# Attention keys loaded ahead of the last projections, output weights loaded in halves and rounded two quarters later, and the last gate row loaded at the fourth tile

## The reference, cut to what matters

```python
mod = jnp.einsum('bd,de->be', c, w_ada[l]) + b_ada[l]
sh1, sc1, gt1, sh2, sc2, gt2 = jnp.split(mod, 6, axis=-1)
h = rmsnorm(x, g_norm_mix[l]) * (1.0 + sc1[:, None, :]) + sh1[:, None, :]
x = x + gt1[:, None, :] * hybrid_mixer(h, positions, w_in[l], w_o[l])
h = rmsnorm(x, g_norm_ffn[l]) * (1.0 + sc2[:, None, :]) + sh2[:, None, :]
x = x + gt2[:, None, :] * hier_moe(h, ...)
...
# hybrid_mixer
proj = jnp.einsum('bsd,de->bse', h, w_in)
y_a = dsa_attention(qa, ka, va, qi, ki, wi)      # 8 heads of 64, top 256 keys of a query
y_b = retention(qb, kb, vb, gb, positions)       # 8 heads of 64, by chunks
y = jnp.concatenate([y_a, y_b], axis=-1)
return jnp.einsum('bse,ed->bsd', y, w_o)
```

## Time and profile before

| | |
|---|---|
| median of three runs | 1718.81 us (1712.06 to 1719.7) |
| the profiled execution's own time | 1713.41 us |
| its span | 1711.5 us |
| TensorE busy | 1473.0 us, 86% |
| VectorE busy | 1125.3 us, 66% |
| ScalarE busy | 912.8 us, 53% |
| GpSimd busy | 286.1 us, 17% |
| granted TensorE clock, mean | 0.926 |
| chain that ended last | TensorE 74%, VectorE 11%, DMA 5%, ScalarE 4% |

### The profile page before, as it was taken

The page is one execution under the profiler, slowest core; times in us unless marked ns, Lnnn a source line. Parts: engine busy times, 40 slices in busy tenths (PEclk is TensorE's granted clock), DMA queues, the critical chain, the costliest instruction groups (busy, mean ns, idle before and its releaser), DMA issues.

```text
span 1711.5 us, 21563 instructions
## 1 busy us (share of the span) xinstructions
PE 1473.0 (86%) x7406; PEld 1149.6 (67%) x7406; DVE 1125.3 (66%) x1496; ACT 912.8 (53%) x1228; POOL 286.1 (17%) x212
## 2 busy tenths in 40 slices
PE   3899998999999897778899752999999999999940
PEld 2587445888887785455666542788888888888830
DVE  6633778662267973334444235899999999999936
ACT  4321665879983112324444301677777777777711
POOL 0000100240000001400000001223223232232125
PEclk8899989999999898599999965999999999999975
DMA  9198532222323226112211104999999999999847
GB/s 370 46 340 316 197 131 105 99 99 99 117 71 128 79 68 222 52 50 74 75 50 44 50 25 148 391 397 398 404 399 398 398 398 400 392 403 395 346 163 269
DMA packets 103990, 368.27 MB, mean 215 GB/s; under 512 B 11248, under 2 KB 24176, under 8 KB 79344
## 3 DMA queue, kind: packets, MB, share of 16 engines
q1 hardware_dynamic: 75632, 291.85, 44.7%
q10 hardware_dynamic: 17024, 41.95, 6.4%
q0 software_dynamic: 11264, 33.57, 5.5%
HBM read 306.50 MB, written 69.21 MB: 220 GB/s over the span
## 4 chain that ended last, share of the span: by engine, by line
PE 74%; DVE 11%; DMA 5%; ACT 4%; issue 3%; POOL 2%; SPq 1%; DVEq 0%; POOLq 0%; ACTq 0%
PE PS L1618 19%; PE PS L1620 19%; PE PS L1619 18%; PE PS L1719 3%; PE PS L1920 2%; PE PS L1743 2%; DMA WK<-in_w_ada 1%; PE PS L1829 1%; PE PS L1816 1%; DVE wlo L1541 1%; DVE WK L1045 1%; PE PS L1704 1%; PE PS L1675 1%; DMA BIG<-in_b_sh 1%; PE PS L1895 1%
## 5 line engine op out<-in xcount | busy, mean ns | idle before, releaser
L1541 DVE TENSOR_TENSOR wlo<-raw,whi 128x2048 fp32r<-128x2048 f32 x192 | 435.9, 2286 | 33.9 <-ACT whi L958 33.5
L958 ACT ACTIVATE whi<-raw 128x2048 fp32r<-128x2048 f32 x192 | 363.9, 1914 | 116.2 <-DVE WK L1560 80.8
L1618 PE MATMUL PS<-whi,xhi 128*128 128x512 f32 x512 | 203.8, 398 | 7.3 <-DVE wlo L1541 6.5
L1620 PE MATMUL PS<-whi,xlo 128*128 128x512 f32 x512 | 201.1, 393 | 0.0
L1619 PE MATMUL PS<-wlo,xhi 128*128 128x512 f32 x512 | 200.1, 391 | 0.0
L850 ACT ACTIVATE KV<-ACC,WK 128x1024 int8<-128x1024 f32 (+4 forms) x160 | 147.5, 925 | 29.9 <-DVE WK L1181 27.3
L1618 PE MATMUL PS<-KVR,BIGR 128*128 128x512 f32 x320 | 127.7, 399 | 5.9 <-DVE KVR L1107 5.9
L699 POOL COPY wcol<-tw 128x1 f32 (+1 forms) x32 | 63.0, 1969 | 376.8 <-DVE WK L1578 376.8
L1620 PE MATMUL PS<-KVR,BIGR 128*128 128x512 f32 x320 | 125.4, 392 | 0.0
L1619 PE MATMUL PS<-KVR,BIGR 128*128 128x512 f32 x320 | 125.0, 391 | 0.0
L1618 PEld LDWEIGHTS PS<-whi,xhi 128*128 128x128 f32 x512 | 97.0, 189 | 27.6 <-issue 5.7
(11 more groups left out here) (322 smaller groups left out, 2966.3 us busy)
## 6 DMA issues: line engine op xcount, KB each, us to landing
raw<-in_w_gate SPq DMA_DIRECT2D x64, 1024.0 KB, 7.8
raw<-in_w_up SPq DMA_DIRECT2D x64, 1024.0 KB, 7.8
raw<-in_w_down SPq DMA_DIRECT2D x64, 1024.0 KB, 7.2
y_dram<-zero ACTq DMA_DIRECT2D x8, 3072.0 KB
WK<-in_w_ada POOLq DMA_DIRECT2D x16, 1024.0 KB, 7.4
y_dram<-WK ACTq DMA_DIRECT2D x32, 512.0 KB
KV<-in_w_in SPq DMA_DIRECT2D x5, 2048.0 KB, 9.8
KV<-in_x SPq DMA_DIRECT2D x16, 512.0 KB, 5.0
```

The source lines that it names most:

```text
L958: nc.scalar.activation(whi[:, slot], raw[:, q], ACT.Copy).then_inc(G("m_hi"), 1)
L1541: V.tensor_tensor(wlo[:, slot], raw[:, q], whi[:, slot].bitcast(F32), ALU.subtract)\
L1618: mm(out_, x_hi, w_hi, start=first, stop=False)
L1620: return mm(out_, x_lo, w_hi, start=False, stop=final)
```

## The change

The keys get the place of the third slot's rounded weights (BIG[20480:24576]), which is free once `ka` is projected, and are loaded in one transfer at step 17; four of the eight rounded slices of `wo` take the keys' old place (`WOR`). The small load of tile 0's keys goes. The output weights come in halves, the second behind `gt1`, and `gt1` has a count of its own; the router's weights move behind the other rows. The first late row stands after quarters 2 and 3 of tile 0 instead of 0 and 1, the second at the first two quarters of tile 1, the third within the first output products. ScalarE rounds slices 4 to 7 in quarters 2 and 3 of tile 0 and 0 to 3 in the first two of tile 1; GpSimd subtracts four slices, VectorE the other four. `gt2` is loaded when the fourth tile begins and made in tile 5. `TILES` is the identity, so the indices that go through it are as before.

```diff
-KEY_PARTS = ((0, 512), (512, 1024))
-KEYS_FROM = {128: 0, 256: 1, 640: 2}
+TILES = (0, 1, 2, 3, 4, 5, 6, 7)
+WO_ORDER = (4, 5, 6, 7, 0, 1, 2, 3)
...
-        wo_hi = [BIGR[:, a:a + 1024] for a in (0, 1024, 2048, 3072, 20480, 21504, 22528, 23552)]
-        kaT = KV[:, 0:4096].rearrange("p (j s) -> p j s", j=4)
+        kaT = BIG[:, 20480:24576].rearrange("p (j s) -> p j s", j=4)
+        wo_hi = [(BIGR, WOR)[k // 4][:, 1024 * (k % 4):1024 * (k % 4) + 1024] for k in range(KD)]
...
-        between[0] = [[("late", m)] for m in range(4)]
-        between[1] = [[("late", 4)], [("late", 5), ("mix", (0, 0))], [("mix", (0, 1))], [("norm", 0)]]
+        between[0] = [[], [], [("late", 0)], [("late", 1)]]
+        between[1] = [[("late", 2)], [("late", 3), ("mix", (0, 0))], [("late", 4), ("mix", (0, 1))],
+                      [("late", 5), ("norm", 0)]]
...
-        between[T - 1][2].append(("late", 6))
-        between[T - 1][3].append(("late", 7))
+        between[5][2].append(("late", 6))
+        between[5][3].append(("late", 7))
... SyncE
+                if step == 2 * T + 1:
+                    for q in range(2):
+                        sp.wait_ge(G(f"st_q{q}"), 16 * T)
+                    sp.wait_ge(G("a_proj"), T * (ATTEND + 2))
+                    sp.dma_start(kaT, k_dram).then_inc(G("ld_k0"), 16)
...
-            for q in range(2):
-                sp.wait_ge(G(f"st_q{q}"), 16 * T)
-            sp.dma_start(keys0, k_dram[:, :, 0:P]).then_inc(G("ld_k0"), 16)
             sp.wait_ge(G("a_proj"), UNITS)
-            for n, (a, b) in enumerate(KEY_PARTS):
-                sp.dma_start(kaT[:, :, a:b], k_dram[:, :, a:b]).then_inc(G(f"ld_k{n + 1}"), 16)
-            sp.dma_start(wo, wo_v).then_inc(G("ld_wo"), 16)
+            sp.dma_start(wo[:, 4:8], wo_v[:, 4:8]).then_inc(G("ld_wo"), 16)
             sp.wait_ge(G("b_y"), T)
-            sp.dma_start(WC["gt1"], b_gt1).then_inc(G("ld_c"), 16)
-            sp.dma_start(WC["wr"], w_router).then_inc(G("ld_c"), 16)
+            sp.dma_start(WC["gt1"], b_gt1).then_inc(G("ld_gt1"), 16)
+            sp.dma_start(wo[:, 0:4], wo_v[:, 0:4]).then_inc(G("ld_wo_last"), 16)
             sp.dma_start(WC["sc2"], b_sc2).then_inc(G("ld_c"), 16)
             sp.dma_start(WC["g"], g_ffn).then_inc(G("ld_c"), 16)
             sp.dma_start(WC["sh2"], b_sh2).then_inc(G("ld_c"), 16)
+            sp.dma_start(WC["wr"], w_router).then_inc(G("ld_c"), 16)
...
-                if i == T - 1:
-                    sp.wait_ge(G("topk_done"), len(SCORED))
+                if i == 3:
                     sp.dma_start(gt2, b_gt2).then_inc(G("ld_gt2"), 16)
... GpSimd
-            for k in range(KD):
-                pool.wait_ge(G("w_hi"), 4 * (ATTEND + 3) + k + 1)
+            for k in range(4, KD):
+                pool.wait_ge(G("w_hi"), 4 * (ATTEND + 3) + WO_ORDER.index(k) + 1)
                 own.go(tt(wo_lo[:, k], wo[:, k], wo_hi[k].bitcast(F32), ALU.subtract), G("wo_lo"))
... ScalarE, at the end of a quarter
-                    if i == 0:
-                        for k in (lo, lo + 1):
-                            act.wait_ge(G("ld_wo"), 16)
+                    quarter = 4 * i + lo // 2
+                    if 2 <= quarter < 6:
+                        for k in WO_ORDER[2 * quarter - 4:2 * quarter - 2]:
+                            act.wait_ge(G("ld_wo" if k >= 4 else "ld_wo_last"), 16)
                             own.go(A(wo_hi[k], wo[:, k], ACT.Copy), G("w_hi"))
... VectorE, at the end of a quarter
+                    quarter = 4 * i + lo // 2
+                    if 4 <= quarter < 6:
+                        for k in (2 * quarter - 8, 2 * quarter - 7):
+                            dve.wait_ge(G("w_hi"), 4 * (ATTEND + 3) + WO_ORDER.index(k) + 1)
+                            own.go(V.tensor_tensor(wo_lo[:, k], wo[:, k], wo_hi[k].bitcast(F32), ALU.subtract),
+                                   G("w_lo"))
                 if kind == "late":
-                    dve.wait_ge(*((G("ld_gt2"), 16) if row == "gt2" else (G("ld_c"), 16 * 5)))
+                    dve.wait_ge(*((G("ld_" + row), 16) if row in ("gt1", "gt2") else (G("ld_c"), 16 * 4)))
... TensorE
                 if lo == 0:
+                    if i == 0:
+                        pe.wait_ge(G("ld_k0"), 32)
                     pe.wait_ge(G(f"ld_q{i % 2}"), 16 * (i // 2 + 1))
-                    if cols_of(i) in KEYS_FROM:
-                        n = KEYS_FROM[cols_of(i)]
-                        pe.wait_ge(G(f"ld_k{n}"), 32 if n == 0 else 16)
```

More of the change, by code:

```diff
@@ L151, in block_kernel @@
         rounded.close()
+        rounded = ExitStack()
+        rounded.enter_context(nc.sbuf_tensor("BIGP", [P, 24576], F32R))
+        WOR = rounded.enter_context(nc.sbuf_tensor("WOR", [P, 4096], F32R))[:, :]
+        rounded.close()
         BIG = sb_before("BIG", [P, 24576])
@@ L509, in load_queries @@
             def load_queries(n):
-                sp.dma_start(queries(n), q_dram[:, :, tile(n)]).then_inc(G(f"ld_q{n % 2}"), 16)
+                sp.dma_start(queries(n), q_dram[:, :, tile(TILES[n])]).then_inc(G(f"ld_q{n % 2}"), 16)
             def store_retained(t):
@@ L1253, in negated_logits @@
                 i = u // HA
-                K = cols_of(i)
-                bias = WC["bias01"][:, 256 - K:256] if i < FIRST_SCORED else ACC[:, ACC_OFF[i]:ACC_OFF[i] + K]
+                n = TILES[i]
+                K = cols_of(n)
+                bias = WC["bias01"][:, 256 - K:256] if n < FIRST_SCORED else ACC[:, ACC_OFF[n]:ACC_OFF[n] + K]
                 b = 2 * (u % 2)
@@ L1360, in _ @@
                     spend(STEP_SPEND, pieces)
-            for _ in pieces:
-                pass
             for kind, i in order:
@@ L1420, in _ @@
                     dve.wait_ge(G("b7_ready"), at7[("route", i, 0)] + 1)
-                    own(V.tensor_copy(L[:, i, :], PS[:, 7, 0:36]), G("b7_free"))
+                    own(V.tensor_copy(L[:, TILES[i], :], PS[:, 7, 0:36]), G("b7_free"))
             dve.wait_ge(G("st_x1"), 16 * T)
@@ L1743, in query_keys @@
                         last = mm(PS[:, 2 * (h % 2) + b, 0:w], queries(i)[rows, h // 2, :],
-                                  (kaT if i else keys0)[rows, h // 2, 512 * b:512 * b + w], start=True, stop=True)
+                                  kaT[rows, h // 2, 512 * b:512 * b + w], start=True, stop=True)
                         if w < 512 or 512 * b + w == K:
@@ L1814, in turn_weights @@
                     pe.wait_ge(G("c_pt"), n - 1)
-                for b in range(4 * g, min(4 * g + 4, i + 1)):
+                for b in range(4 * g, min(4 * g + 4, TILES[i] + 1)):
                     last = tr(PS[:, 4 + n % 2, P * (b % 4):P * (b % 4) + P],
@@ L1829, in values @@
                         last = mm(PS[rows, 6, P * (h // 2):P * (h // 2) + P], va[:, b, HD * h:HD * h + HD],
-                                  PT[(n + h % 2) % 4][:, P * (b % 4):P * (b % 4) + P], start=(b == 0), stop=(b == i))
+                                  PT[(n + h % 2) % 4][:, P * (b % 4):P * (b % 4) + P], start=(b == 0), stop=(b == TILES[i]))
                 last.then_inc(G("c_pv"), 1)
@@ L1881, in _ @@
                         if i == 0 and h == 0:
-                            pe.wait_ge(G("wo_lo"), k + 1)
+                            if k < 4:
+                                pe.wait_ge(G("w_lo"), 4 * (ATTEND + 3) + k + 1)
+                            else:
+                                pe.wait_ge(G("wo_lo"), k - 3)
                         last = split_product(PS[:, 7, :], yhi[:, k, :], ylo[:, k, :], wo_hi[k][:, part], wo_lo[:, k, part],
```

24 lines of the change are left out of this document (12 added, 12 removed).

## The result

| | before | after |
|---|---|---|
| time, median of 4 runs each (us) | 1717.97 (1712.06 to 1719.7) | 1696.29 (1695.42 to 1698.91) |
| the profiled execution's own time | 1713.41 | 1695.42 |
| its span | 1711.5 | 1693.5 |

The ratio is 0.9877, with a 95% interval of 0.9855 to 0.9899: 17 to 25 us less. The two profiled executions are 18.0 us apart.

What follows compares the result with a forecast made beforehand. Bound by bytes in a load queue around tile 0, with a second such place at tile 7. Front 9.7 + tile 7 10.2 - tile 5 1.5 = 18.4 us: 1695.0 profiled, 1700.4 from the median; forecast 1699, range 1690 to 1709.

Steps and rivals of the forecast that it cites:

- Keys at no cost: Retention steps: the early 2 MB key load delays v of step 6 within its slack of 3 us, cost 0.
- The queue: Load queue before tile 0: 6.43 MB instead of 8.53, so rows land at 683.0, gt1 near 672, yb issued about 683.7.
- Lead at the sums of tile 0, 14.0 us: Tile 0, TensorE: the sums of rows start at 688.0 instead of 702.17, about 14.0 us sooner.
- Lead at (mix 0,0), 11.9: First output product, held by VectorE's moved work, starts at 706.3 instead of 718.24, a lead of 11.9 us.
- Late 4 and 5, 2.2: Late rows now behind the first output products cost 2.1 and 0.1 us, leaving a front gain of 9.7.
- Tile 7, 10.2: Gt2's early load removes the wait before tile 7's sums, 9.35 us, plus 0.89 by full clock: mix 10.2 us earlier.
- It also keeps its clock: Tile 7: TensorE stays at full clock, so the sums take 1.09 us instead of 1.98.
- Tile 5, 1.5 (0 to 3.5): Gt2's two late rows, now in tile 5, cost 1.5 us there, between 0 and 3.5.
- Nothing after the first place starts at a fixed time, so the lead is handed on: After the front: each load waits for a tile's count, so the lead reaches the experts undiminished.
- the moved wait: Rival, chance 0.2: subtractions and roundings ahead of late 2 and 3 hold (mix 0,0); front gain 3, total 12, 1706 us.
- the early clock: Rival, chance 0.12: TensorE reaches full clock already in the quarters and late rows, 7 us more gain, 1692 us.
- the queue was the limit: Opposite of a rival, chance 0.05: another wait stands at the same place, total only 6 to 8 us, 1712 us.

Runs made afterwards that it cites:

- gt2 alone: Kernel before with only gt2's bias row loaded at the fourth tile and its two late rows made in tile 5; 1706.94 us, ratio 0.9917.
- rounded early: Changed kernel with output weights rounded in quarters 0 to 3 instead of 2 to 5, VectorE's subtractions in quarters 2 and 3; 1704.83 us, ratio 0.9922.
- GpSimd subtracts all: Changed kernel with all eight weight subtractions on GpSimd and none on VectorE; 1692.93 us, ratio 0.9849.

## Why the prediction was right, step by step

The forecast was 1699 us, by a sum of 1695.0 for a profiled execution that took 1695.42. That closeness is partly luck. From K to R the traces show 15.29 us less (358.61 and 343.32), where the sum had 18.4; K came 0.31 us earlier, and 2.40 us came behind R, where the change does nothing and the traces differ as much among themselves. Without these 2.40 the sum would have been 2.8 us too large.

- **Keys at no cost**: right. No load of v was waited for, and K lies among the others.
- **The queue**: right. Gt1 671.8 (about 672), the last of the four rows 683.3 (683.0), yb 683.95 (683.7). ScalarE waited for no load of output weights.
- **Lead at the sums of tile 0, 14.0 us**: 14.02 by K to sums (35.54 before, 21.52 after).
- **Lead at (mix 0,0), 11.9**: 12.62 by K-M. VectorE was last, as said, for 2.47 us, its subtractions took 1.18 us each (1.22), and GpSimd was through at 690.7 (691).
- **Late 4 and 5, 2.2**: M-S1 grew by 1.65, with the clock up 1.1 us of (mix 0,0) sooner than before (4.2 us into it, before 5.3). Right in mechanism. By S1 the front gain is 10.97 (9.7).
- **Tile 7, 10.2**: 10.45, from S6 to the first product of (mix 7,0) (56.90 before, 46.45 after). Right up to there. "It also keeps its clock" holds for the sums alone: within (mix 7,0) eight products ran at half, in both traces of the changed kernel, and from its first product to R the changed kernel takes 37.86 us, before 36.50. That gives back 1.36.
- **Tile 5, 1.5 (0 to 3.5)**: 2.48 in S4-S6, or 2.87 in gt2 alone. The late rows themselves cost 1.11 of it: so much longer is S4-S6 in the two traces (rounded early and GpSimd subtracts all, 82.55) where the clock stays full there. The other 1.37 are the half-clock stretch behind the sums (2.72 us at 885.27), which the sum did not have; in those two traces one comes in S6-S7 instead (43.68).
- **"Nothing after the first place starts at a fixed time, so the lead is handed on"**: this step failed. The lead of attention went through S1-S2 with 1.75 us less and S2-S4 with 0.54 less: no wait took it, but TensorE's clock. In S1-S2 the same instructions keep TensorE busy for 31.38 us instead of 29.60, most of it within (mix 1,1) (0.83 between 750 and 760; at the same place before, 1.00), and in S2-S4 the sums of tile 2 take 1.97 instead of 1.09.

Of the rivals, the moved wait did not come (K-M is better than forecast), nor the early clock; the queue was the limit. What the prediction did not see is whose the gain is. It put the front down to bytes ahead of the rows, the halves and the later rounding included. By the traces the keys give 4.92 us, gt1's count 3.61, and the rest 4.09 at (mix 0,0), of which S2 shows nothing, 2.4 by the rows that stand there now and 1.8 by the clock.

What stays open: why K moves by 5 us from run to run. The medians differ by 21.7 us where the two traces differ by 18.0. The traced run of before is 4.6 us under its median and the changed one's 0.9, so that difference is the choice of runs. Open is also what decides whether a half-clock stretch comes, and with it how much of the last 4.09 us at (mix 0,0) could be kept.

## What to carry to other kernels

A wait on a count of several loads is a wait for the last: give the row that is wanted first its own count before you split or move the big transfer. Cut a change into its parts and follow each to a place well behind it, as a lead at the next product can be gone two tiles later. And where VectorE and GpSimd share an elementwise step, look whether they run it together: here that took VectorE 2.74 us for a subtraction of 1.18, and the kernel with the lowest median had all of them on GpSimd.
